# Decay products in four row quarters, and differential attention behind even blocks with its steps ordered by kind

## The reference, cut to what matters

```
# differential attention, 8 heads, per block of 128 queries, in each of the two mixers
s = einsum('bqhmd,bkhmd->bhmqk', q_blk, k) * scale       # m = 2 score maps, d = 64
p = softmax(where(mask, s, neg))
a = p[:, :, 0] - lam * p[:, :, 1]
o = einsum('bhqk,bkhe->bqhe', a, v)                      # e = 128
o = rmsnorm(o, diff_ln_g) * (1 - lam_init)

# decays of the linear attention: z_lr = hc @ w_lr, 2 directions x rank 16
z = einsum('bldr,drk->bldk', z_lr, w_alpha) + b_alpha    # k = 4 heads x 64
la = maximum(log_sigmoid(z) / 16, -1)
```

## Time and profile before

| what | value |
|---|---|
| median of 3 runs | 1730.06 us (1729.62 to 1731.22) |
| the profiled execution's own time | 1734.61 us |
| its span | 1732.9 us |
| TensorE busy | 1720.6 us, 99% of the span |
| VectorE, ScalarE, GpSimd busy | 1145.7, 861.3 and 231.0 us |
| granted clock of TensorE, mean | 0.999 |

### The profile page before, as it was taken

How to read it: one execution, slowest core, us unless ns; L and a number is a source line. 1 busy time by engine, 2 the same in 40 slices (tenths; PEclk the granted TensorE clock), 3 DMA queues, 4 the chain that set the end, 5 groups by cost and what they waited for, 6 DMA issues and landing times.

```text
span 1732.9 us, 31049 instructions
## 1 busy us (share of the span) xinstructions
PE 1720.6 (99%) x12693; PEld 1579.1 (91%) x12693; DVE 1145.7 (66%) x1815; ACT 861.3 (50%) x1412; POOL 231.0 (13%) x291
## 2 busy tenths in 40 slices
PE   9999999999999999999999999999999999999999
PEld 9998798999899879998799998999877888979999
DVE  5774658786667566754677777666665747765553
ACT  5444354674444435443544754454436446555543
POOL 2000042221000000000132212000012515210000
PEclk9999999999999999999999999999999999999999
DMA  8676577445657657765676445777535434466653
GB/s 277 220 246 216 180 244 233 153 144 189 204 192 255 222 171 250 255 209 194 209 234 217 134 160 170 248 238 243 177 118 172 103 93 131 146 194 195 195 189 104
DMA packets 257518, 334.71 MB, mean 193 GB/s; under 512 B 15210, under 2 KB 217168, under 8 KB 257376
## 3 DMA queue, kind: packets, MB, share of 16 engines
q1 hardware_dynamic: 251312, 317.42, 56.4%
q0 software_dynamic: 6064, 15.31, 2.7%
HBM read 327.45 MB, written 1.05 MB: 190 GB/s over the span
## 4 chain that ended last, share of the span: by engine, by line
PE 91%; DVE 4%; DMA 2%; ACT 1%; issue 1%; POOL 0%; SPq 0%; POOLq 0%; DVEq 0%; ACTq 0%
PE bank L757 19%; PE bank L760 19%; PE bank L758 19%; PE bank L801 7%; PE bank L802 7%; PE bank L799 7%; DVE wlo L2013 2%; PE bank L923 1%; ACT whi L1571 1%; DMA mtmp<-mtmp 1%; PE bank L773 1%; PE bank L1049 1%; PE bank L883 1%; PE bank L777 1%; PE bank L781 1%
## 5 line engine op out<-in xcount | busy, mean ns | idle before, releaser
L2013 DVE TENSOR_TENSOR wlo<-raw,whi 128x1024 fp32r<-128x1024 f32 x549 | 669.8, 1228 | 335.3 <-ACT whi L1571 331.2
L1571 ACT ACTIVATE whi<-raw 128x1024 fp32r<-128x1024 f32 x549 | 572.1, 1051 | 405.8 <-PE bank L802 217.3
L757 PE MATMUL bank<-XTh,whi 128*128 128x256 f32 x1984 | 555.6, 280 | 0.0
L760 PE MATMUL bank<-XTh,wlo 128*128 128x256 f32 x1984 | 551.6, 278 | 0.5 <-DVE wlo L2013 0.5
L758 PE MATMUL bank<-XTl,whi 128*128 128x256 f32 x1984 | 551.0, 278 | 0.0
L760 PEld LDWEIGHTS bank<-XTh,wlo 128*128 128x128 f32 x1984 | 374.6, 189 | 1.5 <-DVE wlo L2013 1.4
L757 PEld LDWEIGHTS bank<-XTh,whi 128*128 128x128 f32 x1984 | 372.8, 188 | 2.3
L758 PEld LDWEIGHTS bank<-XTl,whi 128*128 128x128 f32 x1984 | 372.9, 188 | 0.0
L757 PE MATMUL bank<-HCh,whi 128*128 128x256 f32 (+2 forms) x864 | 244.3, 283 | 0.0
L758 PE MATMUL bank<-HCl,whi 128*128 128x256 f32 (+2 forms) x864 | 242.2, 280 | 0.0
L760 PE MATMUL bank<-HCh,wlo 128*128 128x256 f32 (+2 forms) x864 | 242.1, 280 | 0.0
(11 more groups left out here) (370 smaller groups left out, 2367.4 us busy)
## 6 DMA issues: line engine op xcount, KB each, us to landing
raw<-in_ffn_w_dram SPq DMA_DIRECT2D x131, 1024.0 KB, 5.2
raw<-in_w_in_dram SPq DMA_DIRECT2D x76, 1024.0 KB, 5.2
raw<-in_w_mod_dram SPq DMA_DIRECT2D x24, 1024.0 KB, 5.1
raw<-in_w_branch_dram SPq DMA_DIRECT2D x16, 1024.0 KB, 5.0
raw<-in_w_out_dram SPq DMA_DIRECT2D x12, 1024.0 KB, 5.0
raw<-in_w_ffn_gate_dram SPq DMA_DIRECT2D x11, 1024.0 KB, 5.1
raw<-in_w_ffn_up_dram SPq DMA_DIRECT2D x11, 1024.0 KB, 5.1
raw<-in_w_ffn_down_dram SPq DMA_DIRECT2D x8, 1024.0 KB, 5.0
```

What stands on the lines that cost most here:

```text
L757: e.matmul(o, hi[:, k, w0:w0 + nc_], xh, start=first and k == 0, stop=False)
L760: m = e.matmul(o, lo[:, k, w0:w0 + nc_], xh, start=False, stop=last and k == nk - 1)
L1571: e.activation(hi_part(n), raw_part(n), ACTF.Copy).then_inc(WHI.did(n), 1)
L2013: e.tensor_tensor(lo_part(n), raw_part(n), hi_part(n).bitcast(F32), ALU.subtract).then_inc(WLO.did(n), 1)
```

## The change

It does two things. The table `ATT` gets other slots and another order: head h has S in 2h, E in 2h+1, T in 2h+4, O in 2h+6, N in 2h+7 and X in 2h+10 (at most 23), and the steps of one slot stand in the order S, E, O, N, X, T. And z is computed four times side by side: the 32 columns of its weight are repeated to 128 in the split, so that z lands in all four quarters of 32 partitions; `WA` holds one 32 x 128 block in each quarter, and each of the four decay products uses the rows of its own quarter.

```diff
-    def chunk_a(w, k0, nk, c0, width=256, bw=128):
+    def chunk_a(w, k0, nk, c0, width=256, bw=128, copies=1):
...
-        chunks.append((src, nk, width, [(slice(0, nk), slice(b, min(b + bw, width)), nk, min(bw, width - b), STANDS)
+        chunks.append((src, nk, width, [(slice(0, nk), slice(b, min(b + bw, width)), nk, copies * min(bw, width - b), STANDS)
...
-    chunk_a(w, 0, 8, 3072, 32)
+    chunk_a(w, 0, 8, 3072, 32, copies=4)
...
-    for _off, _kind in ((0, "S"), (1, "E"), (3, "T"), (4, "O"), (5, "N"), (7, "X")):
-        ATT.setdefault(2 * _h + _off, []).append((_kind, _h))
-ATT = [sorted(ATT.get(_s, []), key=lambda x: x[1]) for _s in range(22)]
+    for _off, _kind in ((0, "S"), (1, "E"), (4, "T"), (6, "O"), (7, "N"), (10, "X")):
+        ATT.setdefault(min(2 * _h + _off, 23), []).append((_kind, _h))
+ATT = [sorted(ATT.get(_s, []), key=lambda x: ("SEONXT".index(x[0]), x[1])) for _s in range(24)]
...
-        ZL = SO[0:32, 0:2, :].rearrange("p a b -> p (a b)")
-        WA = SO[0:32, 2:4, :]
+        ZL = SO[:, 0:2, :].rearrange("p a b -> p (a b)")
+        WA = SO[:, 2, 0:128]
...
+            r = raw[c % 3][:, 0:nk * width].rearrange("p (k c) -> p k c", k=nk)[:, ks, cs]
+            n = hs[j][3] // (cs.stop - cs.start)
+            return r.unsqueeze(2).broadcast_to([128, nk, n, width]) if n > 1 else r
+
+        def in_copies(n, part):
+            _, cs, _, b, _ = chunks[parts[n][0]][3][parts[n][1]]
+            n = b // (cs.stop - cs.start)
+            return part.rearrange("p k (n c) -> p k n c", n=n) if n > 1 else part
...
-                        e.matmul(bank[b][:, :], WA[:, db // 2, (db % 2) * 128:(db % 2) * 128 + 128], ZL, start=True, stop=True).then_inc(
+                        r = slice(32 * db, 32 * db + 32)
+                        e.matmul(bank[b][:, :], WA[r, :], ZL[r, :], start=True, stop=True).then_inc(
...
-                gemm_a(bank[b][0:32, :], xj, "z", nc_=32)
+                gemm_a(bank[b][:, :], xj, "z")
...
-                e.activation(hi_part(n), raw_part(n), ACTF.Copy).then_inc(WHI.did(n), 1)
+                e.activation(in_copies(n, hi_part(n)), raw_part(n), ACTF.Copy).then_inc(WHI.did(n), 1)
...
-                e.activation(ZL, bank[B2["z"]][0:32, :], ACTF.Copy).then_inc(A2.did("z"), 1)
+                e.activation(ZL, bank[B2["z"]][:, :], ACTF.Copy).then_inc(A2.did("z"), 1)
...
-                e.tensor_tensor(lo_part(n), raw_part(n), hi_part(n).bitcast(F32), ALU.subtract).then_inc(WLO.did(n), 1)
+                e.tensor_tensor(in_copies(n, lo_part(n)), raw_part(n), in_copies(n, hi_part(n)).bitcast(F32), ALU.subtract).then_inc(WLO.did(n), 1)
...
-                for d in range(2):
-                    e.dma_start(SO[16 * d:16 * d + 16, 2 + d, :], I["gla_w_alpha_2"][0, d]).then_inc(WAIN.did("wa", by=16), 16)
+                for db in range(4):
+                    d, blk = db // 2, db % 2
+                    at = 32 * db + 16 * d
+                    e.dma_start(WA[at:at + 16, :], I["gla_w_alpha_2"][0, d][:, blk * 128:(blk + 1) * 128]).then_inc(WAIN.did("wa", by=16), 16)
```

More of the change, by code:

```diff
@@ L569, in raw_part @@
             ks, cs = hs[j][0:2]
-            return raw[c % 3][:, 0:nk * width].rearrange("p (k c) -> p k c", k=nk)[:, ks, cs]
+            r = raw[c % 3][:, 0:nk * width].rearrange("p (k c) -> p k c", k=nk)[:, ks, cs]
[5 more added lines that the diff above has]
+            return part.rearrange("p k (n c) -> p k n c", n=n) if n > 1 else part
         def hi_part(n):
```

## The result

The change makes the kernel slower by 1.7%: 1760.2 us (1758.7 to 1764.2, 4 runs) against 1730.6 us (1729.6 to 1735.1), ratio 1.0169, 95% interval 1.0144 to 1.0194. The forecast was 1754.5. The profiled execution took 1764.24 us, 29.6 more than the profiled one of before (1734.61), the same as between the medians (29.6), so the two traces can be set side by side.

A forecast was written before the change was run, and what follows sets the result against it. TensorE's own work, busy 99%, was taken as the bound. Waits 25.7, less old waits 2.2 and decays 2.5, plus clock 3.4, add 24.4 us to the 1730.1 median: 1754.5; own range 1749 to 1759, wider range 1742 to 1765.

The forecast's parts named there:

- The old waits: TensorE's existing waits at O in the attention, expected to go: 1.1 us per mixer, 2.2 us gained in all.
- The chain of 6.15 us: Attention, odd product's end to O through tanh, exponentials, weighing and N: 6.15 us, so O waits 2.36 or 3.41, 25.7 in all.
- half of the waiting is hidden: Rival: ScalarE or VectorE run the odd slot earlier, waits 12.9 us instead of 25.7, time 1738.3, up to 1742; chance 0.1.
- The maxima behind the block's last turn: Attention, VectorE: maxima wait for T at the block's end, 2.3 us later than S alone, at no cost.
- X of the last head right ahead of the branch product: Last head's X moves to slot 23: nothing taken; 0.2 us per mixer if its cover is short.
- the splits: Attention: ScalarE and VectorE have up to four parts of lead and catch up during waits, so no split comes late.
- The clock: TensorE's granted clock falls behind new idle waits, 1.7 us lost per fall: two falls taken, 3.4 us, between 0 and 17.
- the clock falls behind most waits: Rival: 5 to 10 falls of 1.7 us in the attention add 5 to 14 us, giving 1760 to 1768; chance 0.2.
- the pair of slots at 10.1 with the time over 1760: Sign in the changed profile: then the clock is the cause, to be seen as halves of granted clock behind the waits.
- The decays: Four decay products on TensorE run side by side in quarters: 3.63 us becomes 1.1, 2.5 us gained.
- The DMAs: GpSimd's DMAs for the decays become four, the last landing as the first product starts: may cost 0 to 1 us.
- The rival that was not slower: Attention: way to O shorter than 3.79 us, N in time, O not waiting, only gains stay: 1725.4 us; chance 0.08.

## Why the prediction was right, and where it was off

**The bound.** TensorE's own time was the bound: that holds. N is indeed what TensorE would wait for first, but before the change it was in time.

**The old waits, a term that was too large.** The prediction found 0.2 us per pair of slots that its sum of 7.76 did not explain, and called it O coming late; from that came the 2.2 us that were to go. In the trace of before, O at 357.27 starts 0.12 us behind the last matmul of its product, as each matmul of that product does behind the one before it:

```profile
357.15 0.28 PE L760 MATMUL bank<-XTh,wlo 128*128 128x256 f32 x1
...
358.91 0.38 PE L757 MATMUL bank<-XTh,whi 128*128 128x256 f32 x1
```

The missing time is the pace of the products. The one that the 2.74 was taken from lasted 2.85 us; the next one behind scores, from 358.91 to the turn at 361.84, lasted 2.93, with nothing waiting. As waits had 0.4 us, and the two runs without a wait there gained 0.8 and 1.5 us in the two mixers together.

**The chain of 6.15 us.** This is why the forecast came out. Each term was taken from a trace in which the steps stood in another order, and the sum was measured as 6.03. The waits were forecast as eight of 2.36 and two of 3.41, 25.7 us; they were 24.4, with 3.2 for the long ones. Swapping N and E back removed them, filling them left the loop as long, and N first on VectorE alone shortened them by about what the terms say. That is shown, not argued. The rival "half of the waiting is hidden" (12.9 us) falls with the 24.4.

**Nothing else in the attention.** The maxima behind the block's last turn, X of the last head right ahead of the branch product, the splits: none appears in the list of waits, and the slots alone cost nothing.

**The clock, the term that was mis-sized.** Two falls of ten waits, 3.4 us, were taken, "those behind the two longer waits". The profiled execution had four, two of them twice as long, and they cost about 8.5 us (with the old waits' 0.8 to 1.5, the 31.7 us of the mixers leave 8.1 to 8.8). The forecast was 5.2 us low: 5.1 for the clock and about 1 for the old waits, less 1.3 for waits that were taken too long, which makes 4.8. That a fall of 3.4 us at 1.2 GHz comes with an idle wait was right; that one fall of 3.4 is all that a wait brings was not. The wait of 3.2 us had 6.8 us of low clock beside it in both mixers. The argument against more falls, that the new waits stand among dense matmuls and the old one among slow ones, carried no weight: waits of 1.7 us in the run sorted by kind were enough, between the same dense products. And the one wait that the price was read from, 2.3 us in the second block, had no fall in the changed kernel's profile (granted clock 1.00 from 1562.9 to 1566.3), where its list of waits still has it.

So the rival "the clock falls behind most waits" (5 to 10 falls, 1760 to 1768, given 0.2) is what the measured 1760.2 fits. Counted in stretches of 3.4 us the profiled execution had six falls, within its count, though they stood beside four of the ten waits and not most. The forecast's own band, none to four falls and 1749 to 1759, was missed by 1 us; only the wider range, up to 1765, holds the result. The prediction's sign for this case came true as written: the pair of slots at 10.1 with the time over 1760 "is the clock".

**The decays.** The gain of 2.5 was 2.56 on TensorE, with all four quarters together. The run with the decays alone gained 2.4 us in time, with an interval that just includes no gain. The traces show that nothing behind took it back: from about 1320 to 1500 us of the kernel before, the same matmuls keep their distance in the two traces to within 0.05 us. The DMAs cost 0 or 0.6 us, inside the bound. In the changed kernel the first passes of the four products start within two hundredths of a microsecond, and 1.07 us for four is what 1.06 was for two. What the Trainium skill (TensorEngine Tiling (Array Packing), Key Properties) says of tiles that execute in parallel holds here for four tiles of 32 x 128.

**The rival that was not slower** (N in time) fell: it needed the chain to be 2.3 us shorter. It is also the case that N first on both engines reaches, and the time is then near that rival's: 1727.3 against 1725.4, which had the 2.2 us of old waits in it.

## What to carry to other kernels

Sorting the steps of a slot by kind looks neutral when each engine's work stays the same, but in hand-ordered streams the place of a step in its slot is part of its latency. Find, for each buffer that another engine waits for, the step that frees it, and put that step ahead of those whose results are wanted only a slot later. Write the chain down as a sum of rows before moving anything: start to start, on each engine that it crosses.

Where TensorE must wait among dense work, reckon with falls of its clock. Here waits of 1.65 to 3.2 us had falls beside some of them, waits of 0.9 to 1.0 us none, and in the changed kernel the falls cost about a third as much again as the waits. Products that nobody reads were cheaper than standing idle, and having no wait was cheaper still.

Before calling a few tenths of a microsecond a wait, look whether the row in question starts as close behind its predecessor as the rows before it do.

## What the runs showed of the hardware that was not expected

**A wait costs more than itself.** In each mixer of the changed kernel 12 us of waits cost about another 4 us through the clock. The amount is not fixed: there were 20.5 us of low clock in the attention of the changed kernel and 10.2 in the run with the attention alone, which has the same ten waits at the same places. The run sorted by kind had 20.5, with twelve shorter waits, and the one with head 5's waits filled 10.2.

**The matmul has two paces at the same granted clock.** TensorE's counts in a stretch of 40 us within the last feed-forward part, at a granted clock of 1.00, before the change:

```profile
1600.00:1640.00 40.00, 40.00 (x355) 1.00 0.60 188
```

and after it:

```profile
1600.00:1640.00 40.00, 40.00 (x342) 1.00 0.64 202
```

The records are 3.7% fewer for the same code, without a wait: 0.117 instead of 0.113 us from start to start. It holds through the whole of this part. The execution of the kernel with N first had the slow pace here, the one sorted by kind and the one with slots alone the fast one. In the fourth feed-forward part, behind the second mixer, it was the other way round, before the change

```profile
1100.00:1140.00 40.00, 40.00 (x342) 40.00 (x341) 24.81 (x30) 21.25 (x30) 0.00 (x0) 1.00 0.66 216
```

and after it

```profile
1130.00:1170.00 40.00, 40.00 (x355) 40.00 (x354) 25.20 (x31) 21.67 (x31) 0.00 (x0) 1.00 0.69 226
```

Over the last part, some 170 us, this is 5.8 us, more than either gain that this case has to show; it may be part of what spreads the runs of one kernel over 5 to 10 us, which was not looked into. Within the mixers the pace changes inside one execution, as the products of 2.85 and 2.93 us above show, and it explains why the pair of slots with N first was 7.93 and not 7.76. What sets the pace was not tried and stays open.
